# Forming shift times weights on VectorE instead of TensorE, and merging a norm's squares into one tile, at three norms of a two-block network

## The chip, the cores and the metric

One core of one Trainium2 chip runs the whole kernel. The metric is the device time of one execution in microseconds. A TensorE matmul is "PE", its weight load "PEld", VectorE "DVE", ScalarE "ACT", GpSimd "POOL", and SyncE ("SP") issues the weight transfers.

## The reference, cut to what matters

512 tokens of width 1024, in float32, pass through a first block (recurrences, attention, mixture of experts) and a second block of two layers. The change touches only norms of the second block:

```python
for l in range(DEPTH_2):                       # 2 layers
    mod = c_act @ w_ada[l] + b_ada[l]
    sh1, sc1, gt1, sh2, sc2, gt2 = split(mod, N_MOD)
    h = rms_norm(x, norm1[l]) * (1.0 + sc1) + sh1
    proj = h @ w_in[l]
    ...
    x = x + gt1 * (merged @ w_out[l])
    h2 = rms_norm(x, norm2[l]) * (1.0 + sc2) + sh2
    hidden = square(relu(h2 @ w_ff1[l]))
    x = x + gt2 * (hidden @ w_ff2[l])
return rms_norm(x, final_norm)
```

The vectors sh and sc hold one value per channel; with gain = norm * (1 + sc), h @ W = (1/rms) * ((gain * x) @ W) + sh @ W, where rms belongs to the token.

## The kernel before

**Layout.** Activations stand transposed: xT holds x as 8 row tiles of 128 channels x 512 tokens. Every weight matrix comes as slabs of 1 MB: 1024 rows x 256 columns, as 8 row tiles k of 128x256 side by side in one tile of 128x2048. Slabs are counted in pairs m with slots j = 0 and 1. SP loads a slab into raw[j]; ScalarE rounds it to w_hi[j] (L212 to L217); GpSimd forms the remainder w_lo[j] = raw[j] - w_hi[j] (L223 to L227); TensorE multiplies (L272 to L274: w_hi by hi, w_hi by lo, w_lo by hi, for each row tile and each half f of the columns). raw[j] is loaded again once w_lo[j] is formed. Each engine has its own instruction stream, written by hand; semaphores tie them together.

**Norms.** The second block has five norms, u = 2 to 6. u = 2 opens layer 0 and has code of its own, u = 6 ends the kernel. The three between are u = 3 (behind w_out of layer 0), u = 4 (behind the last FF group of layer 0, it opens layer 1) and u = 5 (behind w_out of layer 1). At these three the product that makes x (four slabs, the last one in another order, L374 to L376) is followed by a **raised slab**: slot 0 of pair m+2, multiplied not with the normalised rows but with gain * x, while the norm is still being worked out. Its product is scaled by 1/rms afterwards, and shift @ W is added as a bias.

**Who does what at such a norm.**
- VectorE, `add_raise`: adds each slab's product to xT (L1931), forms the low part of gain * x (L434, behind ScalarE's high part L428), adds up tiles of squares (`norm_add` L362, then L467 and L469, the latter tells `norm_merged`); squares are ScalarE's (L307, L506, L510).
- TensorE, `slabs_to_x`: the raised slab's row tiles; behind k = 2 it sums the merged squares over channels with ones (`token_sums` L339, 4 matmuls for sq[:, 0] and 4 for sq[:, 7] at each norm; the trace shows two records for each of these, hence x16); behind k = 3 it spreads 1/rms over the partitions (`spread_inverse` L347); behind k = 4 come the 16 matmuls of `shift_products` (L412), shift in two parts as the 2-column operand against w_hi and w_lo; at the end `shift_turn` (L421) turns the row by two one-column matmuls.
- ScalarE takes the square root (L317), VectorE the reciprocal (L530). Then `norm_scaled` forms for each of the 8 tiles the normalised tile (L547), whose high part is ScalarE's (L329) and whose low part is VectorE's (L556). At its step 3 `shift_keep` (L448) copies the 2x256 sums out of PSUM; at step 6 `ahead_product` scales the raised product (L452 to L457).
- Behind h_hi tile 5 ScalarE casts slab m+3, 0, and GpSimd forms its remainder.
- The slab behind the raised one (m+2, 1) takes the normalised tiles one by one, waiting for each.
- At u = 4 alone VectorE has three small operations on the next layer's vectors (L2916, L2917, L2919) between `add_raise` and the reciprocal.

```python
                if k == 2:
                    pe.wait_ge(norm_merged, u - 1)
                    token_sums(pe, sq[:, 0], True, False)
                    pe.wait_ge(norm_sq, 4 * u + 4)
                    token_sums(pe, sq[:, 7], False, True).then_inc(norm_sum, 1)
                elif k == 3:
                    spread_inverse(pe, u)
                elif k == 4:
                    shift_products(pe, u - 2)
```

Of the kernel before, what the change touches and what calls it, by code (L numbers as in the profile page):

```python
# [25 lines left out]
ALU = mybir.AluOpType  # L26
# [3 lines left out]
P = 128  # L30
# [3 lines left out]
KT = D // P  # L34
SLAB_COLS = 256
# [112 lines left out]
def build(nc, t):  # L148
    with ExitStack() as whole:
# [7 lines left out]
        def sem(name):  # L157
            return whole.enter_context(nc.semaphore(name))
# [206 lines left out]
        def slabs_to_x(pe, m, hi, lo, ready, u, sq, added, raised=None):  # L365
# [20 lines left out]
            for k in range(KT):  # L386
                pe.wait_ge(ahead_lo, 8 * (u - 2) + k + 1)
                slab_piece(pe, 0, k, *raised)
                if k == 2:
                    pe.wait_ge(norm_merged, u - 1)  # L390
                    token_sums(pe, sq[:, 0], True, False)
                    pe.wait_ge(norm_sq, 4 * u + 4)
                    token_sums(pe, sq[:, 7], False, True).then_inc(norm_sum, 1)
                elif k == 3:
                    spread_inverse(pe, u)
                elif k == 4:
                    shift_products(pe, u - 2)
            shift_turn(pe, u - 2)

# [36 lines left out]

        def shift_vector(dve, v, e, shift):

            if e:
                dve.wait_ge(shift_done, e)  # L440
            v(dve.tensor_copy(shift_parts[:, :, 0], shift))
            dve.tensor_tensor(shift_parts[:, :, 1], shift, shift_parts[:, :, 0].bitcast(F32),
                              ALU.subtract).then_inc(shift_ready, 1)
# [14 lines left out]

        def add_raise(dve, v, at, gate, u, sq, added, hi, lo, gain):

            e = u - 2
            for n in range(3):
                add_to_x(dve, v, at + n // 2, n % 2, 4 * (n // 2), gate)
                raise_vector(dve, e, (2 * n, 2 * n + 1), hi, lo, gain)
            norm_add(dve, u, sq, added, (1,))
            add_to_x(dve, v, at + 1, 1, 4, gate, u - 2, lambda: norm_add(dve, u, sq, added, (2,)))
            v(dve.tensor_tensor(sq[:, 0], sq[:, 0], sq[:, 1], ALU.add))  # L467
            dve.wait_ge(half_sq, u - 2)
            dve.tensor_tensor(sq[:, 0], sq[:, 0], sq[:, 6], ALU.add).then_inc(norm_merged, 1)  # L469
            raise_vector(dve, e, (6, 7), hi, lo, gain)  # L470
# [68 lines left out]
        def norm_scaled(dve, u, sq, gain, shift=None, v=None, m=None):  # L539

            for step in range(KT + 1):
                if m is not None and u > 2 and step == 3:
                    shift_keep(dve, u - 2)
                elif m is not None and step == 6:
                    ahead_product(dve, v, m, u - 2)
# [1231 lines left out]
        O = Y  # L1777
# [76 lines left out]
        def lv_(i):  # L1854
            return lay[:, i:i + 1]
# [167 lines left out]
        def _(pool):  # L2023
# [7 lines left out]
            for l in range(LAYERS):  # L2031
                L = LAYERS_AT + LAYER_PAIRS * l
                if l:
                    remainder(pool, L, 0)
                remainder(pool, L, 1)
# [681 lines left out]
        def _(dve):  # L2717
# [169 lines left out]
            def next_modulation(l):  # L2887
# [23 lines left out]
            for l in range(LAYERS):  # L2911
# [385 lines left out]
```

## Time and profile before

| | |
|---|---|
| median of 3 runs | 2675.76 us (2674.24 to 2678.48) |
| profiled execution | 2674.15 us, span 2672.3 us |
| mean granted TensorE clock | 0.989 |
| PE / PEld busy | 2608.3 us (98%) / 2142.5 us (80%) |
| DVE / ACT / POOL busy | 1500.5 (56%) / 1104.4 (41%) / 873.3 us (33%) |
| slab transfers near the norms | 1024 KB, 5.0 us median from issue to landing |

Busy shares are means over the whole span. A row of a timeline gives start, duration, engine, line, operation, output <- inputs, shape and count, and in square brackets the idle time of the engine ahead of it with its releaser. Matmul rows overlap: a 128x512 matmul is printed with 0.39 us, while the next one starts 0.23 later.

### The profile page before, as it was taken

What the parts mean: (1) busy time and instruction counts of PE and PEld (TensorE: products, weight loads), DVE (VectorE), ACT (ScalarE), POOL (GpSimd) and SP (SyncE); (2) the same over time, 40 slices, a digit from 0 to 9 for tenths busy, and PEclk for the clock granted to TensorE, in tenths of its full rate; (3) what the DMA queues carried; (4) which work ended last, traced back from release to release, by engine and by line L of the source; (5) the groups of instructions that cost most, each with busy time, mean ns of one, the idle gap of its engine ahead of it and who ended that gap; (6) DMA issues with size and microseconds to landing.
All of it is one profiled execution on the core that took longest, in us unless ns stands there. A gap on an engine that the chain in (4) does not pass through costs nothing.

```text
span 2672.3 us, 32709 instructions
## 1 busy us (share of the span) xinstructions
PE 2608.3 (98%) x13070; PEld 2142.5 (80%) x13070; DVE 1500.5 (56%) x1688; ACT 1104.4 (41%) x1295; POOL 873.3 (33%) x199
## 2 busy tenths in 40 slices
PE   7999889999999999999999999999999999999998
PEld 5776778888788888888888888888888888888887
DVE  6574537999754393263564336834563463735445
ACT  5453636787524432343332223435432343422322
POOL 0211020000242443444444444432443454444444
PEclk9999898999999999999999999999999999999999
DMA  4240026999121572233323332322652332233332
GB/s 153 103 151 1 1 101 243 364 366 348 60 96 63 184 273 83 97 111 110 105 102 120 124 131 101 102 95 77 241 202 85 104 119 85 104 127 125 120 123 104
DMA packets 61293, 361.14 MB, mean 135 GB/s; under 512 B 7280, under 2 KB 8176, under 8 KB 26096
## 3 DMA queue, kind: packets, MB, share of 16 engines
q1 hardware_dynamic: 58720, 353.49, 37.0%
q10 hardware_dynamic: 2448, 5.90, 0.7%
q8 instruction: 89, 1.46, 0.2%
q14 instruction: 36, 0.29, 0.0%
HBM read 357.25 MB, written 2.10 MB: 134 GB/s over the span
## 4 chain that ended last, share of the span: by engine, by line
PE 79%; DVE 5%; ACT 2%; issue 1%; ACTq 0%; DVEq 0%
PE pd L272 19%; PE pd L273 19%; PE pd L274 19%; PE pd L296 2%; PE pd L298 2%; PE pd L297 2%; PE pd L2173 2%; PE pd L2175 2%; PE pd L2174 2%; DVE sb_y_lo L1905 2%; DVE sb_h_lo L556 1%; PE pd L2200 1%; PE pd L2202 1%; PE pd L2201 1%; PE pd L2130 1%
## 5 line engine op out<-in xcount | busy, mean ns | idle before, releaser
L226 POOL TENSOR_TENSOR sb_w_lo<-sb_raw,sb_w_hi 128x2048 fp32r<-128x2048 f32 x179 | 836.2, 4672 | 1699.3 <-ACT sb_w_hi L217 1699.3
L272 PE MATMUL pd<-sb_h_hi,sb_w_hi 128*128 128x512 f32 x1600 | 634.5, 397 | 7.5 <-DVE sb_h_lo L556 5.1
L273 PE MATMUL pd<-sb_h_lo,sb_w_hi 128*128 128x512 f32 x1600 | 624.4, 390 | 0.0
L274 PE MATMUL pd<-sb_h_hi,sb_w_lo 128*128 128x512 f32 x1600 | 624.3, 390 | 0.0
L217 ACT CAST sb_w_hi<-sb_raw 128x2048 fp32r<-128x2048 f32 x185 | 353.6, 1912 | 421.3 <-PE pd L274 324.6
L272 PE MATMUL pd<-sb_y_hi,sb_w_hi 128*128 128x512 f32 x960 | 376.5, 392 | 8.0 <-DVE sb_y_lo L1916 3.9
L273 PE MATMUL pd<-sb_y_lo,sb_w_hi 128*128 128x512 f32 x960 | 374.2, 390 | 0.0
L274 PE MATMUL pd<-sb_y_hi,sb_w_lo 128*128 128x512 f32 x960 | 374.1, 390 | 0.0
L272 PEld LDWEIGHTS pd<-sb_h_hi,sb_w_hi 128*128 128x128 f32 x1600 | 301.3, 188 | 76.1 <-issue 6.7
L274 PEld LDWEIGHTS pd<-sb_h_hi,sb_w_lo 128*128 128x128 f32 x1600 | 301.2, 188 | 63.5
L273 PEld LDWEIGHTS pd<-sb_h_lo,sb_w_hi 128*128 128x128 f32 x1600 | 301.2, 188 | 62.4 <-issue 1.9
L272 PEld LDWEIGHTS pd<-sb_y_hi,sb_w_hi 128*128 128x128 f32 x960 | 180.6, 188 | 50.2 <-DVE sb_y_lo L1905 8.4
L274 PEld LDWEIGHTS pd<-sb_y_hi,sb_w_lo 128*128 128x128 f32 x960 | 180.6, 188 | 38.1
L273 PEld LDWEIGHTS pd<-sb_y_lo,sb_w_hi 128*128 128x128 f32 x960 | 180.7, 188 | 36.7
L1905 DVE TENSOR_TENSOR sb_y_lo<-sb_T,sb_y_hi 128x512 fp32r<-128x512 f32 x80 | 187.5, 2383 | 36.6 <-ACT sb_y_hi L1879 29.7
L1931 DVE SCALAR_TENSOR_TENSOR sb_xT<-pd,sb_lay,sb_xT 128x512 f32<-128x512 f32 x80 | 56.8, 747 | 178.6 <-PE pd L274 171.3
L566 DVE CUSTOM_DVE_ANT_0 sb_QK<-sb_QK,sb_Y 128x1024 f32<-128x1024 f32 x32 | 81.2, 2572 | 73.8 <-ACT sb_Y L2597 54.9
L1874 ACT ACTIVATE sb_T<-pd 128x512 f32<-128x512 f32 x60 | 32.6, 596 | 208.0 <-PE pd L274 208.0
L296 PE MATMUL pd<-sb_w_hi,sb_h_hi 128*128 128x512 f32 x288 | 113.6, 394 | 1.1 <-ACT sb_V L2547 1.1
L298 PE MATMUL pd<-sb_w_lo,sb_h_hi 128*128 128x512 f32 x288 | 112.1, 389 | 0.0
L297 PE MATMUL pd<-sb_w_hi,sb_h_lo 128*128 128x512 f32 x288 | 112.1, 389 | 0.0
L3103 DVE TENSOR_TENSOR sb_T<-sb_T 128x512 f32<-128x512 f32 x64 | 41.4, 688 | 107.6 <-ACT sb_T L1874 107.5
(570 smaller groups left out, 3703.0 us busy)
## 6 DMA issues: line engine op xcount, KB each, us to landing
sb_raw<-in_slabs SPq DMA_DIRECT2D x190, 1024.0 KB, 4.9
sb_moe_raw<-in_moe SPq DMA_DIRECT2D x56, 1024.0 KB, 7.1
sb_raw<-in_moe SPq DMA_DIRECT2D x28, 1024.0 KB, 7.1
sb_QK<-in_ada SPq DMA_DIRECT2D x32, 512.0 KB, 5.2
sb_V<-in_ada SPq DMA_DIRECT2D x32, 512.0 KB, 5.6
sb_M<-in_ada SPq DMA_DIRECT2D x16, 512.0 KB, 4.0
sb_Y<-in_ada SPq DMA_DIRECT2D x16, 512.0 KB, 5.5
sb_MG<-in_ada SPq DMA_DIRECT2D x16, 512.0 KB, 5.6
```

Source lines behind the costliest of these rows:

```text
L217: act.copy(w_hi[j][:], raw[j][:]).then_inc(w_hi_ready[j], 1)
L226: pool.tensor_tensor(w_lo[j][:], raw[j][:], w_hi[j][:].bitcast(F32), ALU.subtract).then_inc(w_lo_ready[j], 1)
L272: pe.matmul(out, w_hi[j][:, cols], hi[:, k], start=(k == 0), stop=False)
L273: pe.matmul(out, w_hi[j][:, cols], lo[:, k], start=False, stop=False)
L274: last = pe.matmul(out, w_lo[j][:, cols], hi[:, k], start=False, stop=(k == KT - 1))
L296: pe.matmul(pd[b][:], hi[:, k, toks], w_hi[j][:, cols], start=(k == 0), stop=False)
L297: pe.matmul(pd[b][:], lo[:, k, toks], w_hi[j][:, cols], start=False, stop=False)
L298: last = pe.matmul(pd[b][:], hi[:, k, toks], w_lo[j][:, cols], start=False, stop=(k == KT - 1))
L566: dve.tensor_tensor_reduce(tiles[slot], tiles[slot], row, 1.0, 0.0, ALU.mult, ALU.add, into).then_inc(ada_used, 1)
L1905: dve.tensor_tensor(y_lo[:, bass.ds(2 * n + f, 1)], T[:, tj + f:tj + f + 1], y_hi[:, bass.ds(2 * n + f, 1)].bitcast(F32), ALU.subtract).th ...
L1931: ins = dve.scalar_tensor_tensor(to, bank, lay[:, bass.ds(gate + tile + 2 * j + f, 1)], to, ALU.mult, ALU.add)
L2173: pe.matmul(pd[x % 2][:], hi[:, k], moe_w_hi[s][:, cols], start=(k == 0), stop=False)
```

## The change

At u = 3, 4 and 5: (1) the 16 shift products, the copy of their sums and the two small operations that split the shift into parts are left out. (2) VectorE's new `shift_sum` stands in `add_raise` behind the second slab's tiles: it waits for raw[0] of the raised slab and forms, over the row tiles, shift_row (128x256) = sum over k of raw tile k times shift(k), in eight operations, each behind the last. (3) TensorE's new `shift_total` sums shift_row over its 128 partitions by two one-column matmuls behind the spread. (4) VectorE adds the squares of the last two tiles, sq[:, 7], into sq[:, 0] too, so TensorE has four token-sum matmuls in place of eight. (5) GpSimd waits for the shift sum before the raised slab's remainder, since that frees raw[0]; one pair of slabs is taken out of its FF loop for this. u = 2 keeps the old products. Streams of ScalarE and SP are unchanged.

```diff
                 if k == 2:
                     pe.wait_ge(norm_merged, u - 1)
-                    token_sums(pe, sq[:, 0], True, False)
-                    pe.wait_ge(norm_sq, 4 * u + 4)
-                    token_sums(pe, sq[:, 7], False, True).then_inc(norm_sum, 1)
+                    token_sums(pe, sq[:, 0], True, True).then_inc(norm_sum, 1)
                 elif k == 3:
                     spread_inverse(pe, u)
-                elif k == 4:
-                    shift_products(pe, u - 2)
-            shift_turn(pe, u - 2)
+                    shift_total(pe, u - 2)
...
+        def shift_total(pe, e):
+
+            pe.wait_ge(shift_summed, e)
+            for f in range(2):
+                last = pe.matmul(px[1][:, f:f + 1], shift_row[:, f * P:(f + 1) * P], ones[:, 0:1],
+                                 start=(f == 0), stop=True, skip_group_check=True)
+            last.then_inc(shift_turned, 1)
...
+        def shift_sum(dve, v, m, e, shift):
+
+            dve.wait_ge(raw_loaded[0], 16 * m + 16)
+            part = lambda k: raw[0][:, k * SLAB_COLS:(k + 1) * SLAB_COLS]
+            v(dve.tensor_scalar(shift_row[:], part(0), shift(0), None, ALU.mult))
+            for k in range(1, KT):
+                ins = dve.scalar_tensor_tensor(shift_row[:], part(k), shift(k), shift_row[:], ALU.mult, ALU.add)
+                if k < KT - 1:
+                    v(ins)
+                else:
+                    v(ins, shift_summed, e)
...
             for n in range(3):
                 add_to_x(dve, v, at + n // 2, n % 2, 4 * (n // 2), gate)
                 raise_vector(dve, e, (2 * n, 2 * n + 1), hi, lo, gain)
+                if n == 1:
+                    shift_sum(dve, v, at + 2, e, shift)
...
             dve.wait_ge(half_sq, u - 2)
-            dve.tensor_tensor(sq[:, 0], sq[:, 0], sq[:, 6], ALU.add).then_inc(norm_merged, 1)
+            v(dve.tensor_tensor(sq[:, 0], sq[:, 0], sq[:, 6], ALU.add))
+            dve.wait_ge(norm_sq, 4 * u + 4)
+            dve.tensor_tensor(sq[:, 0], sq[:, 0], sq[:, 7], ALU.add).then_inc(norm_merged, 1)
             raise_vector(dve, e, (6, 7), hi, lo, gain)
...
             for step in range(KT + 1):
-                if m is not None and u > 2 and step == 3:
-                    shift_keep(dve, u - 2)
-                elif m is not None and step == 6:
+                if m is not None and step == 6:
                     ahead_product(dve, v, m, u - 2)
...
                 if l:
+                    pool.wait_ge(shift_summed, 2 * l)
                     remainder(pool, L, 0)
...
-                with pool.Fori(L + L_FF, L + LAYER_PAIRS) as m:
+                pool.wait_ge(shift_summed, 2 * l + 1)
+                for j in range(2):
+                    remainder(pool, L + L_FF, j)
+                with pool.Fori(L + L_FF + 1, L + LAYER_PAIRS) as m:
```

The order of VectorE's instructions at u = 4, from the second slab's tiles (pd2, pd3) to the third slab's (pd0, pd1), before and after. The second column is the line; L1931 became L1948, L434 became L439.

```order
L1931 SCALAR_TENSOR_TENSOR sb_xT<-pd2,sb_lay,sb_xT 128x512
L1931 SCALAR_TENSOR_TENSOR sb_xT<-pd3,sb_lay,sb_xT 128x512
L434 SCALAR_TENSOR_TENSOR sb_x_lo_3842<-sb_xT,sb_next_mod,sb_x_hi_3841 128x512 x2
L1931 SCALAR_TENSOR_TENSOR sb_xT<-pd0,sb_lay,sb_xT 128x512
L1931 SCALAR_TENSOR_TENSOR sb_xT<-pd1,sb_lay,sb_xT 128x512
...
L1948 SCALAR_TENSOR_TENSOR sb_xT<-pd2,sb_lay,sb_xT 128x512
L1948 SCALAR_TENSOR_TENSOR sb_xT<-pd3,sb_lay,sb_xT 128x512
L439 SCALAR_TENSOR_TENSOR sb_x_lo_3842<-sb_xT,sb_next_mod,sb_x_hi_3841 128x512 x2
L446 TENSOR_SCALAR sb_shift_row<-sb_raw0,sb_next_mod 128x256
L448 SCALAR_TENSOR_TENSOR sb_shift_row<-sb_raw0,sb_next_mod,sb_shift_row 128x256 x7
L1948 SCALAR_TENSOR_TENSOR sb_xT<-pd0,sb_lay,sb_xT 128x512
L1948 SCALAR_TENSOR_TENSOR sb_xT<-pd1,sb_lay,sb_xT 128x512
```

The eight operations of the shift sum now stand between the tiles of the second slab and the adds of the third. The same place holds them at u = 3 and 5.

The order of VectorE's instructions a little later at u = 4, from the last add of x to the reciprocal, before and after (sb_Y holds the squares, sb_lay the layer's vectors).

```order
L1931 SCALAR_TENSOR_TENSOR sb_xT<-pd3,sb_lay,sb_xT 128x512
L467 TENSOR_TENSOR sb_Y<-sb_Y 128x512
L469 TENSOR_TENSOR sb_Y<-sb_Y 128x512
L434 SCALAR_TENSOR_TENSOR sb_x_lo_3842<-sb_xT,sb_next_mod,sb_x_hi_3841 128x512 x2
L2916 COPY sb_lay<-sb_v2 128x40
L2917 TENSOR_TENSOR sb_lay<-sb_b_ada,sb_vec 128x16
L2919 SCALAR_TENSOR_TENSOR sb_lay<-sb_lay 128x8
L530 RECIPROCAL sb_T<-sb_T 128x4
...
L1948 SCALAR_TENSOR_TENSOR sb_xT<-pd3,sb_lay,sb_xT 128x512
L484 TENSOR_TENSOR sb_Y<-sb_Y 128x512
L486 TENSOR_TENSOR sb_Y<-sb_Y 128x512
L488 TENSOR_TENSOR sb_Y<-sb_Y 128x512
L439 SCALAR_TENSOR_TENSOR sb_x_lo_3842<-sb_xT,sb_next_mod,sb_x_hi_3841 128x512 x2
L2936 COPY sb_lay<-sb_v2 128x40
L2937 TENSOR_TENSOR sb_lay<-sb_b_ada,sb_vec 128x16
L2939 SCALAR_TENSOR_TENSOR sb_lay<-sb_lay 128x8
L549 RECIPROCAL sb_T<-sb_T 128x4
```

One more add, L488, stands ahead of the low parts; the three small operations and the reciprocal keep their place behind them.

The order of TensorE's matmuls at u = 4 behind row tile 3 of the raised slab, before and after.

```order
L274 MATMUL pd1<-sb_x_hi_3841,sb_w_lo0 128x512
L347 MATMUL px3<-sb_ident,sb_T 128x128 x4
L272 MATMUL pd0<-sb_x_hi_3841,sb_w_hi0 128x512
L273 MATMUL pd0<-sb_x_lo_3842,sb_w_hi0 128x512
L274 MATMUL pd0<-sb_x_hi_3841,sb_w_lo0 128x512
L272 MATMUL pd1<-sb_x_hi_3841,sb_w_hi0 128x512
L273 MATMUL pd1<-sb_x_lo_3842,sb_w_hi0 128x512
L274 MATMUL pd1<-sb_x_hi_3841,sb_w_lo0 128x512
L412 MATMUL px1<-sb_w_hi0,sb_shift_parts 2x256
L412 MATMUL px1<-sb_w_lo0,sb_shift_parts 2x256
...
L275 MATMUL pd1<-sb_x_hi_3841,sb_w_lo0 128x512
L348 MATMUL px3<-sb_ident,sb_T 128x128 x4
L418 MATMUL px1<-sb_ones,sb_shift_row 128x1 x2
L273 MATMUL pd0<-sb_x_hi_3841,sb_w_hi0 128x512
L274 MATMUL pd0<-sb_x_lo_3842,sb_w_hi0 128x512
L275 MATMUL pd0<-sb_x_hi_3841,sb_w_lo0 128x512
L273 MATMUL pd1<-sb_x_hi_3841,sb_w_hi0 128x512
```

Behind the spread two small matmuls came in, and the products with sb_shift_parts behind row tile 4 are gone.

## Rows read from the trace of the kernel before

**Rows 1.** TensorE's timeline at u = 5: start, duration, engine, line, work.

```profile
2305.78 1.84 PE L339 MATMUL px<-sb_ones,sb_Y 128*128 128x1 f32 x16
...
2311.25 0.28 PE L412 MATMUL px<-sb_w_hi,sb_shift_parts 128*2 128x256 f32 x1
...
2313.09 0.40 PE L272 MATMUL pd<-sb_y_hi,sb_w_hi 128*128 128x512 f32 x1
...
2325.14 0.50 PE L272 MATMUL pd<-sb_h_hi,sb_w_hi 128*128 128x512 f32 x1 [0.23 <-DVE sb_h_lo L556]
```

**Rows 2.** The chain of waits at u = 5: start, us, work.

```profile
2313.67 0.32 DVE sb_shift_row L448
```

**Rows 3.** VectorE's timeline at u = 5.

```profile
2282.41 1.42 DVE L434 SCALAR_TENSOR_TENSOR sb_y_lo<-sb_xT,sb_lay,sb_y_hi 128x512 fp32r<-128x512 f32 x2 [0.86 <-ACT sb_y_hi L428]
2291.02 1.41 DVE L1931 SCALAR_TENSOR_TENSOR sb_xT<-pd,sb_lay,sb_xT 128x512 f32<-128x512 f32 x2 [7.19 <-PE pd L274]
...
2297.20 4.22 DVE L362 TENSOR_TENSOR sb_Y<-sb_Y 128x1024 f32<-128x1024 f32 x1
2301.97 0.75 DVE L1931 SCALAR_TENSOR_TENSOR sb_xT<-pd,sb_lay,sb_xT 128x512 f32<-128x512 f32 x1 [0.55 <-PE pd L376]
...
2303.48 0.69 DVE L469 TENSOR_TENSOR sb_Y<-sb_Y 128x512 f32<-128x512 f32 x1
2304.09 1.41 DVE L434 SCALAR_TENSOR_TENSOR sb_y_lo<-sb_xT,sb_lay,sb_y_hi 128x512 fp32r<-128x512 f32 x2
...
2311.60 0.75 DVE L556 SCALAR_TENSOR_TENSOR sb_h_lo<-sb_Y,sb_lay,sb_h_hi 128x512 fp32r<-128x512 f32 x1
...
2320.52 4.57 DVE L556 SCALAR_TENSOR_TENSOR sb_h_lo<-sb_Y,sb_lay,sb_h_hi 128x512 fp32r<-128x512 f32 x1
```

**Rows 4.** GpSimd's timeline at u = 5.

```profile
2284.80 4.61 POOL L226 TENSOR_TENSOR sb_w_lo<-sb_raw,sb_w_hi 128x2048 fp32r<-128x2048 f32 x1 [8.89 <-ACT sb_w_hi L217]
2295.68 4.65 POOL L226 TENSOR_TENSOR sb_w_lo<-sb_raw,sb_w_hi 128x2048 fp32r<-128x2048 f32 x1 [6.27 <-ACT sb_w_hi L217]
2305.88 4.55 POOL L226 TENSOR_TENSOR sb_w_lo<-sb_raw,sb_w_hi 128x2048 fp32r<-128x2048 f32 x1 [5.55 <-ACT sb_w_hi L217]
2319.93 4.61 POOL L226 TENSOR_TENSOR sb_w_lo<-sb_raw,sb_w_hi 128x2048 fp32r<-128x2048 f32 x1 [9.49 <-ACT sb_w_hi L217]
```

**Rows 5.** Groups of instructions by line, VectorE: busy us, mean ns | idle before.

```profile
L2870 DVE SCALAR_TENSOR_TENSOR sb_T<-sb_T,sb_lay,pd 128x256 f32<-128x256 f32 x28 | 13.3, 474 | 0.0
...
L3032 DVE TENSOR_TENSOR sb_lay<-sb_b_ada,sb_vec 128x32 f32<-128x32 f32 x2 | 8.3, 4139 | 0.1
```

**Rows 6.** VectorE's timeline at u = 4.

```profile
1667.85 1.41 DVE L1931 SCALAR_TENSOR_TENSOR sb_xT<-pd,sb_lay,sb_xT 128x512 f32<-128x512 f32 x2 [5.82 <-PE pd L274]
...
1678.94 0.75 DVE L1931 SCALAR_TENSOR_TENSOR sb_xT<-pd,sb_lay,sb_xT 128x512 f32<-128x512 f32 x1 [0.72 <-PE pd L376]
...
1682.68 0.17 DVE L2919 SCALAR_TENSOR_TENSOR sb_lay<-sb_lay 128x8 f32<-128x8 f32 x1
1684.90 0.18 DVE L530 RECIPROCAL sb_T<-sb_T 128x4 f32<-128x4 f32 x1 [2.05 <-ACT sb_T L317]
```

**Rows 7.** GpSimd's timeline at u = 4.

```profile
1663.01 4.60 POOL L226 TENSOR_TENSOR sb_w_lo<-sb_raw,sb_w_hi 128x2048 fp32r<-128x2048 f32 x1 [10.29 <-ACT sb_w_hi L217]
1672.51 4.63 POOL L226 TENSOR_TENSOR sb_w_lo<-sb_raw,sb_w_hi 128x2048 fp32r<-128x2048 f32 x1 [4.91 <-ACT sb_w_hi L217]
1682.85 4.55 POOL L226 TENSOR_TENSOR sb_w_lo<-sb_raw,sb_w_hi 128x2048 fp32r<-128x2048 f32 x1 [5.71 <-ACT sb_w_hi L217]
```

**Rows 8.** TensorE's timeline at u = 4.

```profile
1685.94 1.05 PE L347 MATMUL px<-sb_ident,sb_T 128*128 128x128 f32 x8
```

**Rows 9.** TensorE's timeline in the first block, at its longest wait there.

```profile
721.48 0.50 PE L272 MATMUL pd<-sb_h_hi,sb_w_hi 128*128 128x512 f32 x1 [3.87 <-DVE sb_h_lo L556]
```

**Rows 10.** Windows: us, busy (x instructions) of PE, PEld, DVE, ACT, POOL, PEclk, DMA, GB/s.

```profile
710.00:715.00 5.00, 4.46 (x20) 3.72 (x21) 5.00 (x9) 2.98 (x5) 0.00 (x0) 1.00 0.03 12
723.00:726.00 3.00, 3.00 (x9) 2.33 (x8) 2.83 (x6) 0.00 (x0) 0.00 (x0) 0.52 0.74 306
```

More of the change, by code:

```diff
@@ L197, in build @@
         norm_merged = sem("norm_merged")
+        shift_summed = sem("shift_summed")
         y_val, y_hi_ready, y_ready = sem("y_val"), sem("y_hi_ready"), sem("y_ready")
@@ L435, in raise_vector, with shift_vector @@
                                          ALU.subtract).then_inc(ahead_lo, 1)
-        def shift_vector(dve, v, e, shift):
-            if e:
-                dve.wait_ge(shift_done, e)
+        def shift_sum(dve, v, m, e, shift):
[8 more added lines that the diff above has]
+                    v(ins, shift_summed, e)
+        def shift_vector(dve, v, shift):
             v(dve.tensor_copy(shift_parts[:, :, 0], shift))
@@ L457, in ahead_product, with add_raise @@
                 dve.tensor_tensor(T[:, f], pd[f][:], T[:, 2], ALU.mult).then_inc(ahead_out, 1)
-        def add_raise(dve, v, at, gate, u, sq, added, hi, lo, gain):
+        def add_raise(dve, v, at, gate, u, sq, added, hi, lo, gain, shift):
             e = u - 2
@@ L2892, in next_modulation @@
                                            ALU.add, ALU.mult))
-                shift_vector(dve, v, 2 * l, next_mod[:, 0:8])
             next_modulation(0)
+            shift_vector(dve, v, next_mod[:, 0:8])
             remainder(dve, LAYERS_AT, 0)
@@ L3093, in _ @@
                         remainders(range(0 if i == 1 else 2 * i, 2 * i + 2), yb + Y_MG, h_lo, h_hi, MG)
-                shift_vector(dve, v, 2 * l + 1, lay[:, MOD + 24:MOD + 32])
-                add_raise(dve, v, L + L_WOUT, MOD + 16, 3 + 2 * l, O, 4 * l + 4, y_hi, y_lo, lambda k: lv_(GAIN + 8 + k))
+                add_raise(dve, v, L + L_WOUT, MOD + 16, 3 + 2 * l, O, 4 * l + 4, y_hi, y_lo, lambda k: lv_(GAIN + 8 + k),
+                          lambda k: lv_(MOD + 24 + k))
                 norm_vector(dve, v, 3 + 2 * l, O, lambda k: lv_(GAIN + 8 + k), lambda k: lv_(MOD + 24 + k), L + L_FF)
@@ L3110, in up_down @@
                         next_modulation(l + 1)
-                        add_raise(dve, v, L + L_FF + 4 * q + 2, MOD + 40, 4 + 2 * l, O, 4 * l + 6, x_hi, x_lo, next_gain)
+                        add_raise(dve, v, L + L_FF + 4 * q + 2, MOD + 40, 4 + 2 * l, O, 4 * l + 6, x_hi, x_lo, next_gain,
+                                  lambda k: next_mod[:, k:k + 1])
                         return
```

## The prediction

> **What bounds the kernel.** TensorE is busy for nearly the whole span (table of the profile), so TensorE's own timeline comes first, where a norm ends. Behind the norm of layer 1's w_out (u = 5) it runs the raised slab with 16 token-sum matmuls at 2305.78 and 16 shift products from 2311.25 to 2313.09, and then the slab that needs the normalised rows. That slab stops at its row tile 5 and resumes at 2325.14, 0.23 us after VectorE's L556 wrote h_lo tile 5 [rows 1]. The other two raised norms (u = 3 and 4) show the same stop for the same releaser. So I read next what decides this stop, which I call the gate: the chain of waits runs from the token sums through square root, reciprocal and spread into VectorE's alternation of L547 and L556, with the copy of the shift row, L448, in it for 0.32 [rows 2]. TensorE's slab work is not in that chain. An instruction taken from TensorE behind the sums only lets it reach the gate earlier.
>
> VectorE's and GpSimd's timelines show a second thing. The L556 of tile 5 takes 4.57 us where its like takes 0.75 [rows 3], and GpSimd's remainder runs beside it from 2319.93 for 4.61 [rows 4]. The same holds for L362 (4.22, [rows 3]) beside the remainder at 2295.68. Tiny operations are held as well: a 128x32 add averages 4139 ns [rows 5]. The reciprocal and operations with an operand in PSUM (L547, L1931) are not: at 2305.88 a remainder starts [rows 4], and reciprocal and L547 go through beside it. Where such a VectorE operation runs already, GpSimd waits for its end and goes ahead of the next one. I use this as a rule below.
>
> **The change, part by part.** All against the profiled execution (2674.15 us); the median of the three runs is 1.6 above it.
>
> *TensorE.* Gone per norm: 16 shift products, 1.84 (2311.25 to 2313.09), and half of the token sums, about 0.9 of 1.84 [rows 1]. Over three norms that is 3 x 2.74 = 8.2 us. The shift products lie behind the spread, so by the chain they are worth nothing; the 0.9 lies ahead of the reciprocal, in the chain. The two one-column matmuls move from the slab's end to behind the spread: nothing.
>
> *VectorE's end of the chain.* The copy L448 goes: -0.32 in each norm [rows 2]. Untouched by anything else, a gate would come 0.9 + 0.32 = 1.2 earlier.
>
> *VectorE, the shift sum.* Eight dependent operations on 128x256. Nearest rows: 0.474 for the same operation on the same shape with one operand in PSUM [rows 5]; below, half of the 0.69 that a 512-column add takes [rows 3], 0.35. I take 0.47, the same shape and form, and 0.04 between dependent ones: 8 x 0.51 = 4.1. For u = 5 it starts where L434 ends, 2282.41 + 1.42 = 2283.83, in VectorE's 7.19 of idle time before the add at 2291.02 [rows 3]. This would cover it, were there no remainder at 2284.80 [rows 4]. Two or three operations are done by then; the others wait until about 2289.9 and end near 2292.3. Queued behind them: the add, 1.2 late; then ScalarE's raised tiles and cast, so the remainder of the raised slab starts 1.2 late (2295.68 to 2296.9, end 2301.6). GpSimd's new wait is met before, at 2292.3, and costs nothing (the pair taken out of its loop is the same work); TensorE wants that slab 2301.7 and is not delayed. SP's queue is unchanged in order; only the next load of raw[0] is asked for 1.2 later, long before its cast, which stands behind h_hi tile 5 on ScalarE.
>
> *Passing it on.* L362 at 2297.20 ended 1.1 after the remainder at 2295.68; now it ends near 2302.7, so the last add of w_out starts 0.75 later than 2301.97 [rows 3]. The new add of the last squares is another 0.69 + 0.04 [rows 3], and both lie ahead of norm_merged: near 2305.65, when TensorE asks at 2305.78 [rows 1]. Just in time. L434 of tiles 6 and 7 moves from 2304.09 to 2305.6, its second half to 2306.25. The remainder of 2305.88 comes 0.75 later too, 2306.63 [rows 4], finds that half running, waits for it, and ends near 2311.5. The first L556, due 0.9 before 2311.60 [rows 3], is held to that end: of the 0.9 only 0.1 to 0.2 stays. With the copy: **-0.5**. The norm u = 3, behind the w_out of layer 0, has the same spacing: **-0.5**.
>
> *u = 4, at the end of layer 0's last FF group.* The spacing is tighter. The shift sum there starts at 1667.85 - 5.82 = 1662.03 [rows 6] beside a remainder from 1663.01 [rows 7], and by the same count ends at 1670.1, where the add stood at 1667.85: 2.2 late. The raised slab's remainder goes from 1672.51 to 1674.7 [rows 7], L362 behind it ends 1680.4, and the last add moves from 1678.94 [rows 6] by 1.6; with the new add, L434 of tiles 6 and 7 runs 1683.45 to 1684.8. The next remainder, at 1682.85 before [rows 7], is also 1.6 later, waits for L434 and runs 1684.8 to 1689.4. Three small operations on the layer's vectors (L2916 to L2919) stand between L434 and the reciprocal. Before, the last of them started at 1682.68, 0.17 ahead of the remainder [rows 6, 7]. The new add alone, 0.73, pushes them behind it, and they are of the kind that is held. So they end at 1689.9, the reciprocal comes at 1690.0 instead of 1684.90, and the spread, which TensorE ran at 1685.94 [rows 6, 8], near 1690.3: +4.3, less the copy's 0.32: **+4.0**. Were the shift sum not late, the remainder would end at 1687.4 and the gate come 1.8 later; did the three pass, 1.2 earlier.
>
> *The clock.* TensorE will stand at u = 4 for some 4.4 us before the spread, and 2.3 at the other gates (it arrives 2.7 earlier, the gate comes 0.5 earlier). The one like it is a wait of 3.87 that ended at 721.48 [rows 9]; the granted clock then fell to the lower level, 1.2 GHz, for a few matmuls: 0.52 over 723 to 726, with 9 matmuls where 3.00 / 0.23 = 13 fit [rows 10], some 1.6 us lost by the end of that stretch. Ahead of that wait TensorE had worked only 4.46 of 5.00 us [rows 10]; ahead of these it has not paused. I take 0 and keep 1.6 for each in the range.
>
> Sum: -0.5 + 4.0 - 0.5 = **+3.0**: 2677.2 for the profiled execution, **2678.8** for the median.
>
> On the length of the eight operations the Trainium skill, "VectorE: DVE Perf Modes", section "The TRN2 errata", has a rule: 58 cycles and one per column at 0.96 GHz for operands in SBUF, an estimate of 0.33 us here. By the same rule a 512-column L556 would be 0.59, and the row says 0.75 [rows 3], so the measurement is the longer one; the sum by the rule is that of F.
>
> **The rivals.**
> B, nothing gets late: the shift sum's operations are not held by the remainder, and the three small ones pass. Each gate -1.2: -3.7, 2672.1. For it: not every small operation was held (L2916 ran 0.17 long, but with no remainder running). Against: the 4139 ns [rows 5].
> F, the summing operations are quicker, 0.35: four instead of three are done before the remainder takes over, the add is 0.4 late at u = 5 and 3, 1.7 at u = 4: -1.0 x 2 + 3.3 = +1.3, 2677.1. For it: all operands in SBUF; against: L556's 0.75.
> C, all that TensorE is freed of counts: -8.2, 2667.6. It needs the gate to move by 2.7 in each norm, so a h_lo tile 5 that is not held; TensorE's busy share speaks for it, the 4.57 of L556 [rows 3] against it.
> D, on the other side: the clock falls behind all three new waits. 3.0 + 3 x 1.6 = +7.8, 2683.6. It needs the two waits of 2.3 to act like the one of 3.87. For it: 721.48 [rows 9]; against: TensorE's unbroken work before. [...]
> E, also slower: at u = 3 and 5 the remainder of 2306.63 gets in ahead of L434's tile 7, which it misses by 0.4 in my sum. Tile 7 and the reciprocal behind it wait until 2312.0 instead of 2307.9, the gates come 2.9 later: 2 x 2.9 + 4.0 = +9.8, 2685.6. It decides from 0.4 more lateness in VectorE against ScalarE.
> That the change does something else is no rival: the order of instructions shows the sum, the add and the missing products at all three norms.
>
> **The numbers.** A, my forecast: 0.50. B 0.14, F 0.04, C 0.12, D 0.11, E 0.09. A alone spans 2675 (no lateness at u = 4: -0.5 + 1.8 - 0.5 = +0.8, less some tenths) to 2680.4 (clock falls once). The range leaves out C and E: 2671.5 to 2684.0. With 0.2% as 5.35 us, about what a measurement can tell: faster is below 2670.4, C and the edge of B, 0.14; slower is above 2681.1, D, E and the edge of A, 0.23; the rest, 0.63, is no change.
>
> **What would show it.** In the changed kernel: shift sum with two or three operations ahead of the remainder and one of over 4 us; the add behind it about 1 to 2 late; at u = 4 one of the small operations before the reciprocal near 4.5 long and a TensorE wait of 4 us at L348; at u = 3 and 5 a wait of about 2.3 for h_lo tile 5, which starts within 1 us of its old place. Wrong would be: a shift sum of eight short operations beside a remainder (B), no wait at tile 5 (C), PEclk under 1 behind the waits (D), a reciprocal after 2311 at u = 5 (E).

## The result and the profile after

Timed on the same chips, the changed kernel takes 2680.62 us (median of 12 runs, 2675.66 to 2683.64), the kernel before 2674.62 (12 runs, 2673.58 to 2678.48). The ratio is 1.0015, 95% interval 1.0008 to 1.0022: 4.0 us slower (2.1 to 5.9). Single executions spread by several us, so the estimate depends on how they are summed up: the two medians lie 6.0 apart, the two means 4.3. The forecast was +3.0, no change by more than 0.2%.

The two profiled executions differ by more, 2679.2 to 2672.3 in span. To see where, I take the start times of one kind of matmul, w_hi by hi (L272 and L374 before, L273 and L375 after), which both traces hold 2656 times, and compare the same one in both. The changed kernel is 2.7 behind at the 233rd already (703.75 against 701.06) and no more at the 921st (1319.87 against 1317.19): that part arose in the first block, where nothing was changed and single executions differ (two versions built from the kernel before, e3 and e9 below, have their 921st at 1316.75 and 1319.90). Three stages hold the rest: from the 921st to the 981st matmul lies u = 3, from the 1431st to the 1491st u = 4, from the 2131st to the 2191st u = 5. Each took 46.7 before; now **+0.6, +3.5 and +0.6**, in sum +4.7. Between and behind them nothing over 0.2 moves.

TensorE's timeline of the changed kernel: the sums, spread and turn of u = 5, and the waits of over 0.3 us at the three norms (u = 3, u = 4 three times, u = 5).

```profile
1347.75 0.50 PE L273 MATMUL pd<-sb_h_hi,sb_w_hi 128*128 128x512 f32 x1 [2.28 <-DVE sb_h_lo L573]
...
1682.57 0.50 PE L273 MATMUL pd<-sb_x_hi,sb_w_hi 128*128 128x512 f32 x1 [0.52 <-POOL sb_w_lo L227]
...
1692.87 1.16 PE L348 MATMUL px<-sb_ident,sb_T 128*128 128x128 f32 x8 [3.67 <-DVE sb_T L549]
...
1708.85 0.50 PE L273 MATMUL pd<-sb_h_hi,sb_w_hi 128*128 128x512 f32 x1 [0.50 <-DVE sb_h_lo L573]
...
2312.73 0.95 PE L340 MATMUL px<-sb_ones,sb_Y 128*128 128x1 f32 x8
2315.02 1.05 PE L348 MATMUL px<-sb_ident,sb_T 128*128 128x128 f32 x8
2315.91 0.50 PE L418 MATMUL px<-sb_ones,sb_shift_row 128*128 128x1 f32 x4
...
2331.11 0.50 PE L273 MATMUL pd<-sb_h_hi,sb_w_hi 128*128 128x512 f32 x1 [2.31 <-DVE sb_h_lo L573]
```

Half of the token sums and all shift products are gone, as in the diff. What TensorE was freed of shows as waiting: 2.3 at u = 3 and 5 where [rows 1] has 0.23, and 3.67 at the spread of u = 4, where it did not wait before. At u = 4 it also waits 0.52 for the remainder of the raised slab, which is now late; the spread behind waits far longer, so this adds nothing here.

VectorE's timeline at u = 4, from the shift sum to the reciprocal.

```profile
1664.92 0.35 DVE L446 TENSOR_SCALAR sb_shift_row<-sb_raw,sb_next_mod 128x256 f32<-128x256 f32 x1
1665.31 7.84 DVE L448 SCALAR_TENSOR_TENSOR sb_shift_row<-sb_raw,sb_next_mod,sb_shift_row 128x256 f32<-128x256 f32 x7
1673.18 1.41 DVE L1948 SCALAR_TENSOR_TENSOR sb_xT<-pd,sb_lay,sb_xT 128x512 f32<-128x512 f32 x2
...
1683.63 0.75 DVE L1948 SCALAR_TENSOR_TENSOR sb_xT<-pd,sb_lay,sb_xT 128x512 f32<-128x512 f32 x1
...
1685.87 0.69 DVE L488 TENSOR_TENSOR sb_Y<-sb_Y 128x512 f32<-128x512 f32 x1
1686.48 1.41 DVE L439 SCALAR_TENSOR_TENSOR sb_x_lo<-sb_xT,sb_next_mod,sb_x_hi 128x512 fp32r<-128x512 f32 x2
1687.80 4.51 DVE L2936 COPY sb_lay<-sb_v 128x40 f32<-128x40 f32 x1
1692.23 0.17 DVE L2937 TENSOR_TENSOR sb_lay<-sb_b_ada,sb_vec 128x16 f32<-128x16 f32 x1
1692.43 0.17 DVE L2939 SCALAR_TENSOR_TENSOR sb_lay<-sb_lay 128x8 f32<-128x8 f32 x1
1692.63 0.18 DVE L549 RECIPROCAL sb_T<-sb_T 128x4 f32<-128x4 f32 x1
```

GpSimd's timeline at u = 4.

```profile
1665.98 4.80 POOL L227 TENSOR_TENSOR sb_w_lo<-sb_raw,sb_w_hi 128x2048 fp32r<-128x2048 f32 x1 [10.01 <-ACT sb_w_hi L218]
1677.91 4.61 POOL L227 TENSOR_TENSOR sb_w_lo<-sb_raw,sb_w_hi 128x2048 fp32r<-128x2048 f32 x1 [7.12 <-ACT sb_w_hi L218]
1687.54 4.73 POOL L227 TENSOR_TENSOR sb_w_lo<-sb_raw,sb_w_hi 128x2048 fp32r<-128x2048 f32 x1 [5.03 <-ACT sb_w_hi L218]
```

The shift sum takes 8.2 us, since a remainder begins at 1665.98 and one of the eight operations waits for its end. The trace is 3.21 later here than that of before (1431st matmul: 1675.09 against 1671.87). Less this, the add behind the shift sum comes 2.1 late, the last add (1683.63) 1.5. Then the copy of 128x40 values, L2936, takes 4.51: the remainder of 1687.54 had gone ahead of it. In the kernel before, the same copy ran ahead of the remainder of 1682.85 [rows 7] (VectorE's timeline):

```profile
1682.39 0.18 DVE L2916 COPY sb_lay<-sb_v 128x40 f32<-128x40 f32 x1
```

So the copy stood 0.46 ahead of the remainder and now stands 0.26 behind it: 0.72 apart, the new add L488 (0.69) and the gap behind it. The lateness of the last add does not count for this, since the remainder starts 3.91 behind it in both kernels (1678.94 to 1682.85, 1683.63 to 1687.54). The reciprocal stands behind the copy, and TensorE's spread behind that.

VectorE's timeline at u = 5.

```profile
2290.69 0.35 DVE L446 TENSOR_SCALAR sb_shift_row<-sb_raw,sb_lay 128x256 f32<-128x256 f32 x1
2291.07 7.83 DVE L448 SCALAR_TENSOR_TENSOR sb_shift_row<-sb_raw,sb_lay,sb_shift_row 128x256 f32<-128x256 f32 x7
2298.94 1.41 DVE L1948 SCALAR_TENSOR_TENSOR sb_xT<-pd,sb_lay,sb_xT 128x512 f32<-128x512 f32 x2
...
2309.41 0.75 DVE L1948 SCALAR_TENSOR_TENSOR sb_xT<-pd,sb_lay,sb_xT 128x512 f32<-128x512 f32 x1
...
2313.91 0.18 DVE L549 RECIPROCAL sb_T<-sb_T 128x4 f32<-128x4 f32 x1 [0.25 <-ACT sb_T L318]
...
2317.65 1.02 DVE L573 SCALAR_TENSOR_TENSOR sb_h_lo<-sb_Y,sb_lay,sb_h_hi 128x512 fp32r<-128x512 f32 x1
...
2326.52 4.53 DVE L573 SCALAR_TENSOR_TENSOR sb_h_lo<-sb_Y,sb_lay,sb_h_hi 128x512 fp32r<-128x512 f32 x1
```

GpSimd's timeline at u = 5.

```profile
2313.31 4.81 POOL L227 TENSOR_TENSOR sb_w_lo<-sb_raw,sb_w_hi 128x2048 fp32r<-128x2048 f32 x1 [5.03 <-ACT sb_w_hi L218]
2325.93 4.57 POOL L227 TENSOR_TENSOR sb_w_lo<-sb_raw,sb_w_hi 128x2048 fp32r<-128x2048 f32 x1 [7.81 <-ACT sb_w_hi L218]
```

At this place the trace is 6.95 later than that of before (2131st matmul: 2299.12 against 2292.18). Less this, the add behind the shift sum comes at 2291.99 against 2291.02 in [rows 3], 1.0 late, the last add at 2302.46 against 2301.97, and h_lo tile 5 begins at 2319.57 against 2320.52, nearly 1 earlier. It is held as before, beside the remainder of 2325.93.

Windows behind the three waits in the changed kernel: us, busy (x instructions) of PE, PEld, DVE, ACT, POOL, PEclk, DMA share, GB/s.

```profile
1349.00:1352.00 3.00, 3.00 (x9) 2.35 (x8) 2.75 (x6) 1.33 (x3) 0.00 (x0) 0.54 0.72 303
1695.00:1698.00 3.00, 3.00 (x10) 2.36 (x9) 2.87 (x5) 1.95 (x3) 0.00 (x0) 0.60 0.99 356
2332.00:2335.00 3.00, 3.00 (x10) 2.30 (x8) 2.76 (x5) 1.46 (x3) 0.00 (x0) 0.55 0.77 306
```

The granted clock falls to its lower level, 1.2 GHz (a PEclk of 0.50), behind each. So at u = 3 and 5 the gate comes 1.0 earlier and the slab behind it loses 1.6: +0.6.

### The profile page after: what moved, and what is told of

Same layout as the page of the kernel before. It is cut to its first block, busy times and chain, and to the rows that moved or that the text cites. A ratio compares the mean times of both kernels' runs of the same rounds, so it can differ in the third digit from the quotient of the medians.

```text
span 2679.2 us, 32586 instructions
## 1 busy us (share of the span) xinstructions
PE 2606.2 (97%) x12998; PEld 2142.2 (80%) x12998; DVE 1529.5 (57%) x1706; ACT 1104.4 (41%) x1295; POOL 873.9 (33%) x199
## 4 chain that ended last, share of the span: by engine, by line
PE 77%; DVE 6%; ACT 2%; issue 1%; POOL 0%; DMA 0%; ACTq 0%; DVEq 0%; SPq 0%; POOLq 0%
PE pd L273 19%; PE pd L275 19%; PE pd L274 19%; PE pd L297 2%; PE pd L299 2%; PE pd L298 2%; PE pd L2196 2%; PE pd L2194 2%; PE pd L2195 2%; DVE sb_y_lo L1922 1%; DVE sb_h_lo L573 1%; PE pd L2221 1%; PE pd L2223 1%; PE pd L2222 1%; PE pd L2151 1%
## 5 line engine op out<-in xcount | busy, mean ns | idle before, releaser
L273 PE MATMUL pd<-sb_h_hi,sb_w_hi 128*128 128x512 f32 x1600 | 636.0, 398 | 11.9 <-DVE sb_h_lo L573 9.5
L273 PE MATMUL pd<-sb_y_hi,sb_w_hi 128*128 128x512 f32 x960 | 376.8, 393 | 8.1 <-DVE sb_y_lo L1933 3.9
L273 PEld LDWEIGHTS pd<-sb_h_hi,sb_w_hi 128*128 128x128 f32 x1600 | 302.2, 189 | 80.9 <-DVE sb_h_lo L573 10.6
L273 PEld LDWEIGHTS pd<-sb_y_hi,sb_w_hi 128*128 128x128 f32 x960 | 180.9, 188 | 50.8 <-DVE sb_y_lo L1922 8.4
L1948 DVE SCALAR_TENSOR_TENSOR sb_xT<-pd,sb_lay,sb_xT 128x512 f32<-128x512 f32 x80 | 56.8, 747 | 155.7 <-PE pd L275 152.0
```

The lines of the kernel that those rows point to most:

```text
L273: pe.matmul(out, w_hi[j][:, cols], hi[:, k], start=(k == 0), stop=False)
L1948: ins = dve.scalar_tensor_tensor(to, bank, lay[:, bass.ds(gate + tile + 2 * j + f, 1)], to, ALU.mult, ALU.add)
```

## The experiments

Two theories are tested: **H**, that the gates hang on VectorE's operations held by GpSimd's remainders, and **K**, that a TensorE wait costs the clock behind it. The table gives each kernel's three stages as differences from 46.7 in its own profile, the stretch between u = 3 and u = 4 (981st to 1431st matmul, 307.95 before), and the timing against runs of the kernel before on the same chip.

| kernel | u = 3 | between | u = 4 | u = 5 | sum | ratio, 95% interval |
|---|---|---|---|---|---|---|
| changed | +0.57 | -0.03 | +3.53 | +0.63 | +4.7 | 1.0015, 1.0008 to 1.0022 |
| e1_lay_early | -0.99 | +0.47 | +1.59 | +0.62 | +1.7 | 1.0000, 0.9991 to 1.0009 |
| e2_filler | -0.92 | -0.09 | +6.06 | -0.95 | +4.1 | 1.0017, 1.0008 to 1.0026 |
| e3_sums_alone | -0.91 | +0.04 | +3.66 | -0.91 | +1.9 | 1.0005, 0.9996 to 1.0014 |
| e4_no_products | +1.57 | +0.06 | -0.02 | +1.51 | +3.1 | 1.0008, 0.9999 to 1.0017 |
| e5_sums_lay | -0.88 | +0.54 | -0.89 | -0.88 | -2.1 | 0.9996, 0.9987 to 1.0005 |
| e7_no_merge | +1.23 | -0.06 | +0.56 | +1.23 | +3.0 | 1.0013, 1.0004 to 1.0023 |
| e8_lay_cast | -2.29 | +0.42 | -1.23 | -2.26 | -5.4 | 0.9983, 0.9974 to 0.9992 |
| e9_before_cast | -0.53 | +0.01 | -0.49 | -0.48 | -1.5 | 0.9993, 0.9984 to 1.0002 |
| e10_sums_lay_cast | -1.38 | +0.50 | -1.36 | -1.37 | -3.6 | 0.9990, 0.9981 to 0.9999 |
| e11_one_of_eight | -2.54 | +0.25 | -2.51 | -2.53 | -7.3 | 0.9974, 0.9965 to 0.9983 |

The stages of one profile are sharp, the timings are not: single executions of every version spread by several us. The sum, which takes in the column "between", lies inside the interval of the timing in all rows. Each version has one profile; a gain or loss of under about 2 us is read from its stages alone.

**Is it the small operations at u = 4?** The copy, the add and the gain go into a function, which is called ahead of add_raise:

```diff
                     if last_group and l + 1 < LAYERS:
                         next_modulation(l + 1)
+                        layer_vectors(l + 1)
                         add_raise(...)
...
-                dve.tensor_copy(lay[:, 0:V2_COLS], v2[:, bass.ds(l, 1)])
+                if l == 0:
+                    layer_vectors(l)
```

> The changed kernel with the three small operations on the next layer's vectors at u = 4 moved ahead of add_raise. Theory H (held operations): the copy of 4.51 us before the reciprocal is gone, the reciprocal comes about 4.5 us earlier, the first low part is then held to the remainder's end, so the gate of u = 4 comes 3.7 to 4.0 earlier. TensorE no longer waits 3.7 us at the spread, but arrives early at tile 5 and waits 2 to 2.5 there; if such waits cost the clock (theory K), 1.6 come back, net 2.1 to 2.4 faster than the changed kernel, some 2676 to 2677 where before is 2674.6; without K 2674.5. Rival (the wait at the spread comes from the late token sums, not from the small operations): same as the changed kernel, the spread still near 5 us behind the sums.

The spread of u = 4 no longer waits, and the gate there is 3.5 earlier than in the changed kernel. TensorE's wait moved on to tile 5, and the clock fell behind it. TensorE's timeline at u = 3 and 4, and windows behind both:

```profile
1349.86 0.50 PE L273 MATMUL pd<-sb_h_hi,sb_w_hi 128*128 128x512 f32 x1 [2.32 <-DVE sb_h_lo L573]
...
1706.35 0.50 PE L273 MATMUL pd<-sb_h_hi,sb_w_hi 128*128 128x512 f32 x1 [2.53 <-DVE sb_h_lo L573]
```

```profile
1350.50:1353.50 3.00, 3.00 (x15) 2.45 (x14) 2.75 (x5) 1.46 (x3) 0.00 (x0) 1.00 0.92 336
1707.00:1710.00 3.00, 3.00 (x8) 2.30 (x7) 2.73 (x6) 0.71 (x1) 0.00 (x0) 0.50 0.87 319
```

At u = 3 a wait of 2.32 did not cost the clock, at u = 4 one of 2.53 did. So the fall is not certain at this length. The move itself costs 0.5 ahead of the norm (column "between"), which I had not expected. Nearly all of it arises at one matmul, where TensorE waits for GpSimd's remainder (TensorE's timeline of e1):

```profile
1671.84 0.50 PE L375 MATMUL pd<-sb_y_hi,sb_w_hi 128*128 128x512 f32 x1 [0.28 <-POOL sb_w_lo L227]
```

The three small operations now stand ahead of the adds of x, and this remainder comes 0.5 later than in the changed kernel; that the adds pass the delay on through ScalarE's cast is argued, not tested.

**Does the waiting cost the clock?** Sixteen matmuls that nobody uses go back behind row tile 4:

```diff
+                elif k == 4:
+                    for n in range(KT):
+                        for w in (w_hi[0], w_lo[0]):
+                            pe.matmul(px[2][0:2, 0:SLAB_COLS], shift_parts[:, n], w[:, n * SLAB_COLS:(n + 1) * SLAB_COLS],
+                                      start=(n == 0 and w is w_hi[0]), stop=(n == KT - 1 and w is w_lo[0]))
```

> The changed kernel with 16 matmuls of the old shape put back behind row tile 4, their sums used by nobody. Theory K (a TensorE wait of over 2 us costs the clock): at u = 3 and 5 the wait at tile 5 falls from 2.4 to about 0.6 us, the granted clock stays at 1.00 behind it and the gate stands where it stood, so 1.6 us less at each of them; at u = 4 the wait before the spread stays, the clock still falls, and the 1.84 of matmuls show as about 1.2 more. Net about 2 us faster than the changed kernel, though TensorE has 5.5 us more to do. Rival (TensorE's work counts): 5.5 us slower. No clock effect: 0 at u = 3 and 5.

At u = 3 and 5 TensorE does 1.8 us more and the stage is 1.5 and 1.6 shorter: K holds there. TensorE's timeline at u = 3, and windows behind u = 3, behind the spread of u = 4 (two lines) and behind u = 5:

```profile
1344.71 0.50 PE L273 MATMUL pd<-sb_h_hi,sb_w_hi 128*128 128x512 f32 x1 [0.49 <-DVE sb_h_lo L578]
```

```profile
1345.50:1348.50 3.00, 3.00 (x14) 2.43 (x13) 2.75 (x5) 1.46 (x3) 0.00 (x0) 1.00 0.73 306
1689.00:1692.00 3.00, 3.00 (x14) 2.81 (x13) 1.51 (x3) 0.86 (x2) 0.00 (x0) 0.50 0.85 318
1692.00:1694.50 2.50, 2.50 (x10) 1.54 (x9) 2.50 (x4) 1.25 (x2) 0.00 (x0) 0.50 0.88 315
2330.00:2333.00 3.00, 3.00 (x15) 2.46 (x14) 2.75 (x5) 1.46 (x3) 0.00 (x0) 1.00 0.75 309
```

The net gain was forecast at 2 and is mostly not there: the stages give 0.6, the timing (1.0017 against 1.0015) nothing. At u = 4 the wait of 3.67 remains. Behind it TensorE has more to do, and the lower clock lasts longer than in the changed kernel (0.50 still from 1692 to 1694.5), so TensorE came later than the gate: +6.1 where I had 4.7.

**The opposite: TensorE's work taken away and nothing put in.** In the kernel before, 15 of the 16 shift products are left out at the three norms:

```diff
-            for k in range(KT):
-                for part in (w_hi[0], w_lo[0]):
+            for k in range(KT) if e == 0 else (KT - 1,):
+                for part in (w_hi[0], w_lo[0]) if e == 0 else (w_lo[0],):
```

> The kernel before with 15 of the 16 shift products left out at u = 3, 4 and 5 (so the shift's part of the raised product is not formed there); nothing is put in their place. Theory H: the gates don't move, TensorE waits about 2.0 us at each tile 5; no gain. With theory K the granted clock falls behind each wait and the kernel is up to 3 x 1.6 = 4.8 slower. Rival (TensorE's freed work counts): 5.2 faster.

The gates lie within 0.03 of their old places, TensorE waits 1.93 at each, and at two of the three the clock falls (windows behind u = 3, 4, 5):

```profile
1349.00:1352.00 3.00, 3.00 (x9) 2.32 (x8) 2.88 (x5) 1.22 (x2) 0.00 (x0) 0.50 0.73 306
1706.50:1709.50 3.00, 3.00 (x15) 2.51 (x14) 2.77 (x5) 0.06 (x1) 0.00 (x0) 1.00 0.73 309
2329.00:2332.00 3.00, 3.00 (x9) 2.33 (x8) 2.75 (x5) 1.45 (x3) 0.00 (x0) 0.55 0.79 322
```

Leaving out 5.2 us of matmuls made no norm shorter and two of them 1.5 to 1.6 longer. Rival C is out.

**The merge of the squares, alone and undone.** First the kernel before with the merge alone (the two hunks on token_sums and on norm_merged), then the changed kernel without it.

> The kernel before with only the added merge of the last squares (VectorE one add more, TensorE four token sums fewer). Theory H: the gates of u = 3 and 5 come 0.85 earlier each; at u = 4 the add alone pushes the three small operations behind the remainder, so a copy of about 4.5 us shows, the spread comes 2.5 later, and so the gate, 1.6 more if the clock falls behind TensorE's wait of some 3.4 us. Net +0.8 to +2.4 against before. Rival (u = 4 suffers only from the late shift sum): no held copy, all three gates 0.85 earlier, -2.5.

> The changed kernel without the merge of the last squares (TensorE sums them again, 8 matmuls). Theory H: at u = 3 and 5 the gate comes only 0.3 earlier than before (the copy of the shift row), with a TensorE wait of some 1.8 us; at u = 4 the three small operations come some 0.1 to 0.3 ahead of the remainder again and pass, the slab starts 0.65 late, gate +0.3. Sum of the gates -0.3, plus up to 1.6 at each norm where the clock falls. Rival (the late shift sum alone pushes the small operations behind the remainder): u = 4 is still 3.5 late.

Both came as theory H has it, within 0.3 at each gate and at the spread. Alone, the merge brings 0.9 at u = 3 and 5 and loses 3.7 at u = 4, where the copy is held with no shift sum in the program (VectorE's timeline of e3; the spread comes 2.2 late, and the clock falls behind TensorE's wait of 2.97 there):

```profile
1681.81 4.51 DVE L2916 COPY sb_lay<-sb_v 128x40 f32<-128x40 f32 x1
```

Without the merge, the shift sum as late as in the changed kernel, u = 4 is only 0.6 longer: the small operations pass, the copy ahead of the remainder of 1685.61 (VectorE's and GpSimd's timelines of e7).

```profile
1685.14 0.18 DVE L2936 COPY sb_lay<-sb_v 128x40 f32<-128x40 f32 x1
```

```profile
1685.61 4.56 POOL L227 TENSOR_TENSOR sb_w_lo<-sb_raw,sb_w_hi 128x2048 fp32r<-128x2048 f32 x1 [5.02 <-ACT sb_w_hi L218]
```

The merge's 0.7 us ahead of the small operations decides u = 4, not the shift sum. At u = 3 and 5 the gate comes 0.34 earlier (the copy of the shift row), TensorE waits 2.05, the clock falls: +1.2. At u = 4 it waits as long, and the clock stays.

**The merge with the small operations out of the way.**

> The kernel before with the added merge of the last squares and with the three small operations of u = 4 moved ahead of add_raise; TensorE keeps its shift products. Theory H: all three gates 0.85 to 0.9 earlier, no TensorE wait over 0.5 us at the norms and so no fall of the clock there: -2.6 against before. Rival (the merge itself delays u = 4): u = 4 stays 2.5 to 3.7 late, as with the merge alone.

Each norm is 0.9 shorter, TensorE's waits are 0.23 to 0.24 and the clock does not fall. With the 0.5 that the move costs the sum is -2.1. The timing (0.9996) can't tell this from nothing.

**Moving the gate.** h_lo tile 5 is held by a remainder that begins behind ScalarE's cast. With the changed kernel and the move of e1 the cast goes one row tile earlier:

```diff
-                if k == (5 if u == 2 else 6) and slab_behind is not None:
+                if k == 5 and slab_behind is not None:
                     split(act, slab_behind, 0)
+                if k == (5 if u == 2 else 6) and slab_behind is not None:
                     slab_out_raised()
```

> The changed kernel with the three small operations moved ahead of add_raise and with ScalarE's cast of the slab behind (m+3, 0) one row tile earlier at the three norms, ahead of h_hi tile 5. Theory H: GpSimd's remainder, which holds h_lo tile 5, starts and ends 1.3 earlier, so the gates come 2.2 (u = 3, 5) and 1.2 (u = 4) earlier than before, the TensorE wait there falls to some 1.2 us, the clock stays: -5.7 against before, some 2669 to 2670. What TensorE was freed of is then worth something. Rival (the gate hangs on VectorE's own sequence, not on the remainder): gates as without the move. Rival on the clock: up to 1.6 comes back at each norm.

> The kernel before with ScalarE's cast of slab m+3, 0 one row tile earlier alone. The cast then waits for TensorE to release the raised slab's w_hi, so it gains 0.6 at most, and TensorE's wait for tile 5 was only 0.23 there: -0.2 in each norm, -0.7 in all, no change that a timing can tell. Rival (the remainder's start alone sets the time): -1.3 in each norm, -3.9.

GpSimd's remainder, VectorE's tile 5 and TensorE at u = 5 in e8_lay_cast:

```profile
2319.85 4.61 POOL L227 TENSOR_TENSOR sb_w_lo<-sb_raw,sb_w_hi 128x2048 fp32r<-128x2048 f32 x1 [6.49 <-ACT sb_w_hi L218]
```

```profile
2321.76 3.26 DVE L574 SCALAR_TENSOR_TENSOR sb_h_lo<-sb_Y,sb_lay,sb_h_hi 128x512 fp32r<-128x512 f32 x1
```

```profile
2325.07 0.50 PE L273 MATMUL pd<-sb_h_hi,sb_w_hi 128*128 128x512 f32 x1 [1.01 <-DVE sb_h_lo L574]
```

Tile 5 now takes 3.26 in place of 4.53, TensorE waits 1.0, and the clock stays. This version beats the kernel before, 2671.17 against 2675.17 on one chip (0.9983), and so the changed kernel, whose ratio is 1.0015. The same move in the kernel before gives 0.5 a norm (I had 0.2): TensorE no longer waits at tile 5 there, so an earlier gate is worth nothing more. The timing (0.9993) can't tell this from nothing.

**What the shift sum is worth, and what its lateness costs.** e10 is the kernel before with the merge and both moves, so shift products on TensorE; e11 is e8 with seven of the eight operations of the shift sum left out.

> The kernel before with the merge of the last squares, the small operations moved and the cast one row tile earlier, but with TensorE's shift products kept and no shift sum. Theory H: the gate comes 0.9 + 0.4 earlier, TensorE, which has only 0.85 less to do, arrives with no wait left over 0.3: -1.4 in each norm, -4.1 in all, 1.6 less than the version with the shift sum and the same two moves, whose surplus is what the shift sum is worth once the gate has moved. Rival (the shift sum is worth nothing on VectorE): the same or better than that version, -5.8.

> The changed kernel with both moves (small operations, cast), and with seven of the eight operations of the shift sum left out, so the shift's part of the raised product is not the right one. Theory H: nothing before the norm is late any more; u = 3 and 5 stay at -2.3, since the lateness was hidden there, u = 4 goes from -1.2 to -2.2: -6.8 in all. Rival (the lateness costs at all three): u = 3 and 5 gain 1 more as well.

With the gate moved, the shift sum on VectorE is worth 0.9 at u = 3 and 5 (-2.3 against -1.4) and costs 0.1 at u = 4: 1.8 in the stages, which the timings (0.9983 and 0.9990) don't separate. The lateness costs 1.3 at u = 4 and, against my forecast of none, 0.25 at the others.

## Why the prediction was right, and where not

- **The gates, right in kind.** TensorE's 8.2 us did not count, as e4 shows without the rest of the change. The place that decides u = 4, a copy held behind a remainder, was named with its size: 4.51 measured. Forecast +4.0 for the gate of u = 4, measured +3.5 (TensorE's wait at the spread 3.67 in place of 4.4). One reading was wrong without harm: the 0.23 of [rows 1] is TensorE's idle time at the gate, not the time since the write, which ended 0.05 before (2320.52 + 4.57 in [rows 3]).
- **The shift sum.** Forecast: 0.51 an operation, two or three done before the remainder, 8.5 from start to end at u = 5. Measured: 0.485 and a gap of 0.04, three done, 8.2. F falls: the estimate of 0.33 by the Trainium skill's rule ("VectorE: DVE Perf Modes", "The TRN2 errata") comes near only the first operation (0.35), which has one tensor operand; of the seven with two, those that are not held take 0.485. B falls: one of the eight was held in each norm.
- **u = 3 and 5: the sum of the gate was off by 0.5.** I had the first low part held to 2311.5 and -0.5; it was held by only 0.27 (1.02 for 0.75), and the gate came 1.0 earlier. VectorE was 0.5 late at the last add and not 0.75, so the remainder ended 0.3 sooner than forecast (2318.12 less 6.95 is 2311.17). And the held operation ended 0.55 behind the remainder, where I had counted a whole one of 0.75. That TensorE's wait still came out at the forecast 2.3 is luck: it reached the gate about 3.05 earlier than before, not 2.7.
- **The step that failed is the clock.** "I take 0 and keep 1.6 for each in the range", since TensorE had not paused ahead of these waits. It fell behind all three waits of the profiled execution, by 1.6 at u = 3 and 5. At u = 4 it cost nearly nothing: the fall came behind the spread, and TensorE still reached the gate 0.50 before it opened. So D's mechanism is there, on top of A's: -1.0 + 1.6 twice and +3.5. The stages, +4.7, lie between A's +3.0 and D's +7.8. Errors of opposite sign kept the total within 1.7 of A, which is luck: at u = 3 and 5 the gate came 0.5 earlier than forecast and the clock cost 1.6 (-0.5 forecast, +0.6 measured), at u = 4 the gate came 0.5 earlier.
- **E** did not occur: the reciprocal of u = 5 ran at 2313.91, less 6.95 at 2306.96, and was not held.
- **The span of A** mixes two bases: its lower end, 2675, counts from the profiled execution, its upper end, 2680.4, from the median. From the median the lower end is 2676.6.

Over all profiles, at the three norms: behind 17 waits of 0.2 to 1.2 us at a gate the clock never fell; behind 11 of 1.9 to 2.6 it fell 8 times; behind three of 3.0 to 3.7 (at the spread, e2, e3 and the changed kernel) each time. The Trainium skill, "TensorE: Matmul & The Clock Gate", "HAM oscillation", also has idle gaps drop the clock, but warns only of longer gaps than most of those that cost it here; where they differ, these rows decide. Why a wait of the same length sometimes passes these runs don't tell. The executions of one version differ in granted clock too: of the 33 of the kernel before that were timed beside e1 to e4, the ten at 0.989 have a median of 2674.7, the fourteen at 0.987 one of 2678.5. Which waits lie behind that was not looked into.

## What to carry to other kernels

An engine that is busy 98% of the time gains nothing from less work if a gate further on is set by another engine. Ask first what opens the gate, and move that together with the work: 15 products less gave +3.1 alone, and with the gate moved, taking all sixteen off TensorE was worth 1.8 (e8 against e10). Where two engines hold one another and the order is fixed, tenths decide: before adding 0.7 us to a queue, look at which small operation behind it now meets the other engine's long one. And a wait that seems free, since another engine sets the pace, can cost 1.5 to 1.6 us here, as the clock may fall behind it.

## What the runs showed of the hardware that I had not expected

Waits as short as 1.93 us were followed by a fall to the lower clock, at a price of 1.5 to 1.6 us each, and sixteen useless matmuls (e2_filler) took that price away at two norms. A 128x40 copy from SBUF to SBUF takes 0.18 us free and 4.51 beside a remainder, in three programs (the changed kernel, e2 and e3) to the same hundredth. A last add of x that comes late moves this copy and the remainder alike (the remainder starts 3.91 us behind it before and after the change); only one more operation in between changed which comes first.
